# Seven half-size products for the Fourier half of an output projection, and reciprocal columns as matmul weights, in a two-block transformer kernel

## The reference, cut to what matters

```python
def second_block(x, c, ctx, c_ctx, norm_g, w_ada, b_ada, w_in, w_four, q_norm_g, k_norm_g, rel_bias, w_out):
    ...
        f_out = _fourier(fx_in, w_four[l]) * jax.nn.silu(fx_gate)
        na_out = _neighbourhood_attention(qx, kx, vx, kc, vc, rel_bias[l]) * jax.nn.silu(nx_gate)
        x_new = x + g_x * (jnp.concatenate([f_out, na_out], axis=-1) @ w_out[l])
```

## Time and profile before

| what | us |
|---|---|
| median of 3 runs (901.07 to 902.05) | 901.18 |
| profiled execution, its own time | 901.18 |
| its span, first to last instruction | 899.4 |
| TensorE busy | 887.7 (99%) |
| VectorE busy | 386.4 (43%) |
| ScalarE busy | 213.6 (24%) |
| GpSimd busy | 172.2 (19%) |
| step 4 of attention two, on TensorE | 816.1 to 829.7 |
| step 8's end, first product of the other half | 872.0 |

### The profile page before, as it was taken

One profiled execution on the slowest core, in us unless ns is written; L12 is line 12 of the kernel. 1 busy time (PEld: TensorE's weight loads), 2 busy tenths in 40 slices (PEclk: granted clock), 3 DMA queues, 4 the chain that ended last, 5 costly groups with the idle time before them and its releaser, 6 DMA issues.

```text
span 899.4 us, 13457 instructions
## 1 busy us (share of the span) xinstructions
PE 887.7 (99%) x5562; PEld 502.7 (56%) x5562; DVE 386.4 (43%) x814; ACT 213.6 (24%) x468; POOL 172.2 (19%) x160
## 2 busy tenths in 40 slices
PE   9999999999999989999999999999999999999998
PEld 5588875455565543333333333344688888866553
DVE  2764543357764346310310310048635542354456
ACT  2211213345544310010110110115201111643420
POOL 3212220000002044140230200033201303191000
PEclk9999999999999999999999999999999999999999
DMA  9945559124010738999999999961382102700002
GB/s 329 326 113 188 188 181 391 60 94 188 1 47 9 271 125 331 405 413 429 423 420 428 420 430 426 401 239 47 110 163 96 51 24 68 249 11 1 2 1 93
DMA packets 54830, 184.28 MB, mean 205 GB/s; under 512 B 15049, under 2 KB 15717, under 8 KB 48497
## 3 DMA queue, kind: packets, MB, share of 16 engines
q1 hardware_dynamic: 46368, 162.41, 48.0%
q0 software_dynamic: 4912, 14.18, 4.3%
q10 hardware_dynamic: 3488, 6.82, 2.0%
HBM read 168.70 MB, written 16.79 MB: 206 GB/s over the span
## 4 chain that ended last, share of the span: by engine, by line
PE 90%; DVE 3%; DMA 2%; ACT 2%; POOL 1%; issue 1%; SPq 0%; DVEq 0%; ACTq 0%; POOLq 0%
PE psum L981 20%; PE psum L1185 18%; PE psum L1206 9%; PE psum L1083 6%; PE psum L885 6%; PE psum L1031 4%; PE psum L1008 4%; PE psum L1457 3%; PE psum L1337 2%; PE psum L1299 2%; PE psum L1045 2%; PE psum L1062 2%; PE psum L1406 2%; PE psum L1110 2%; PE psum L944 1%
## 5 line engine op out<-in xcount | busy, mean ns | idle before, releaser
L1185 PE MATMUL psum<-ring,buf_a 128*32 128x512 f32 x1536 | 166.4, 592 | 1.6 <-issue 1.6
L1185 PEld LDWEIGHTS psum<-ring,buf_a 128*32 128x32 f32 x1536 | 51.6, 110 | 112.8 <-issue 112.8
L1206 PE MATMUL psum<-ring,buf_c 128*32 128x512 f32 x768 | 84.1, 593 | 0.0
L2718 POOL DMA_INDIRECT buf_b<-xq_d,o_sb x48 | 52.6, 1096 | 157.5 <-DVE buf_a L2300 125.1
L2649 POOL TENSOR_TENSOR qk_st<-qk_st,half 128x8 f32<-128x8 f32 x26 | 43.6, 1677 | 160.2 <-DVE qk_st L2384 74.5
L2325 DVE TENSOR_TENSOR buf_c<-buf_c,psum 128x512 f32<-128x512 f32 x12 | 13.1, 1093 | 141.0 <-PE psum L1185 141.0
L981 PE MATMUL psum<-ring,buf_a 128*128 128x256 f32 x320 | 70.9, 380 | 0.0
L981 PE MATMUL psum<-ring,buf_b 128*128 128x256 f32 x288 | 64.8, 380 | 0.0
L981 PEld LDWEIGHTS psum<-ring,buf_a 128*128 128x128 f32 x320 | 60.1, 190 | 8.2 <-issue 0.4
L1948 DVE TENSOR_TENSOR s_buf<-s_buf,psum 128x512 f32<-128x512 f32 x52 | 35.3, 685 | 61.2 <-PE psum L981 58.7
L981 PEld LDWEIGHTS psum<-ring,buf_b 128*128 128x128 f32 x288 | 53.9, 190 | 7.5 <-issue 0.6
(11 more groups left out here) (319 smaller groups left out, 1229.9 us busy)
## 6 DMA issues: line engine op xcount, KB each, us to landing
ring<-in_moe_w_gate SPq DMA_DIRECT2D x16, 2048.0 KB, 13.7
ring<-in_moe_w_up SPq DMA_DIRECT2D x16, 2048.0 KB, 14.8
ring<-in_moe_w_down SPq DMA_DIRECT2D x16, 2048.0 KB, 13.9
ring<-in_w_in SPq DMA_DIRECT2D x7, 2048.0 KB, 12.5
ring<-in_w_ada SPq DMA_DIRECT2D x6, 2048.0 KB, 9.8
ring<-in_da_w_in SPq DMA_DIRECT2D x5, 2048.0 KB, 14.4
y_d<-ring POOLq DMA_DIRECT2D x1, 5632.0 KB, 22.0
y_d<-buf_b ACTq DMA_DIRECT2D x11, 512.0 KB, 11.5
```

The source lines that it names most:

```text
L1185: last = mm(buf("mm", n)[rows, :], x_part[:, j, k, :], slot(moe_load(q, m, r))[:, k, :], start=(k == 0), stop=(k == KD - 1))
L1206: last = mm(buf("sc", n)[rows, m, :], hidT[:, s % 3, f * P + SUB * j:f * P + SUB * (j + 1)], slot(moe_load(q, 2, r), FC)[:, f, m * CH:(m + ...
L2718: pool.indirect_dma_start(out=xg[:, s % 2, j * 256:(j + 1) * 256], out_offset=None, in_=xn_quarters, in_offset=bass.IndirectOffsetOnAxis(a ...
```

## The change

The Fourier half of the projection gets the same seven products as the other half. Six of them (`OUT_F`) take the places of the pieces of three tiles, two in each of the steps 4, 5 and 6; the seventh (S4 times B22) takes the place of the last tile, one matmul in each of the four pieces of two. The sums of inputs are made by VectorE in step 3, behind the last piece of `mixT` and ahead of `diag` 1; the sums of weights by GpSimd at the same signal, `drained` of `fourier` 4 and 5. VectorE adds the products to the quarters of `x`: twelve instructions of 128 x 1024 in place of four, and one more that makes u2 out of the first product, which ScalarE has copied, and the fourth. The diagonal matrix is gone: `spread` now takes the reciprocal of one head as a 128 x 64 weight (one column, repeated) and the identity as the moving matrix, in eight matmuls of 128 columns in place of two of 512.

```diff
 BEFORE_PT = [[], [("fourier", 2)], [("fourier", 4)], [("fourier", 5)],
-             [("out_f", 0)], [("out_f", 1)], [("out_f", 2)], [("out_last", 0)], []]
+             [("out_f", 0)], [("out_f", 2)], [("out_f", 4)], [("out_last", 0)], []]
 AMID_PT = [[("fourier", 1)], [("fourier", 3)], [("fourier_rest", 4)], [("fourier_rest", 5)],
-           [("out_f_rest", 0)], [("out_f_rest", 1)], [("out_f_rest", 2)], [("out_last", 1)], []]
+           [("out_f", 1)], [("out_f", 3)], [("out_f", 5)], [("out_last", 1)], []]
+OUT_F = [("A11", "B11"), ("A12", "B21"), ("S3", "T3"), ("S2", "T2"), ("A22", "T4"), ("S1", "T1")]
...
+        def out_f(i):
+            n = turn["sc", "out_f", i]
+            left, right = OUT_F[i]
+            claim(pe, "sc", n)
+            if i == 2:
+                pe.wait_ge(s_f_ready, 1)
+                pe.wait_ge(t_f_ready, 2)
...
+            for a in range(2):
+                for k in range(2):
+                    last = mm(buf("sc", n)[:, a, :], mix_f[left][:, k, a * P:(a + 1) * P], w_out_f[right][:, k, :],
+                              start=(k == 0), stop=(k == 1))
+            fill(last, "sc", n)
...
         def out_last(piece):
...
-            for i in range(*OUT_LAST[piece]):
-                a, k = divmod(i, 4)
-                last = mm(buf("sc", n)[:, a, :], mixT[:, k, t * P:(t + 1) * P], gated_chunk(a)[:, k, :],
-                          start=(k == 0), stop=(k == 3))
+            a, k = divmod(piece, 2)
+            last = mm(buf("sc", n)[:, a, :], mix_f["S4"][:, k, a * P:(a + 1) * P], w_out_f["B22"][:, k, :],
+                      start=(k == 0), stop=(k == 1))
...
                 elif name == "spread":
...
-                    for hh in range(2):
-                        last = mm(buf("tp", n)[hh * DH:(hh + 1) * DH, :], ones[:, 0:DH],
-                                  o_sb[:, hh * 512:(hh + 1) * 512], start=True, stop=True)
+                    for g in range(4):
+                        for hh in range(2):
+                            last = mm(buf("tp", n)[hh * DH:(hh + 1) * DH, g * P:(g + 1) * P],
+                                      rden[:, m % 2, 2 * g + hh:2 * g + hh + 1].to_broadcast([P, DH]), ident[:], start=True, stop=True)
...
+                elif name == "out_f" and m == 0:
+                    act.wait_ge(f_added, 1)
+                    n = turn["sc", "out_f", 0]
+                    S.copy(f_p1, buf("sc", n)).then_inc(f_p1_copied, 1)
...
+        def sum_f(n):
+            left, right, op = {1: ("A21", "A22", ALU.add), 2: ("S1", "A11", ALU.subtract),
+                               3: ("A11", "A21", ALU.subtract), 4: ("A12", "S2", ALU.subtract)}[n]
+            if n == 2:
+                dve.wait_ge(s_f_ready, 2)
+            elif n == 4:
+                dve.wait_ge(s_f_ready, 3)
+            V.tensor_tensor(mix_f[f"S{n}"], mix_f[left], mix_f[right], op).then_inc(s_f_ready, 1)
...
+            elif i == 3:
+                dve.wait_ge(f_p1_copied, 1)
+                drain(V.tensor_tensor(f_u2, f_p1, product, ALU.add), "sc", n)
...
+            elif i == 5:
+                dve.wait_ge(f_added, 5)
+                add_to("x22", product).then_inc(f_added, 1)
+                drain(add_to("x12", product), "sc", n)
...
                 elif name == "fourier_rest":
...
+                    if m == 5:
+                        drained(dve, "sc", turn["sc", "fourier", 4])
+                        drained(dve, "sc", turn["sc", "fourier", 5])
+                        for sum_of in (3, 1, 2, 4):
+                            sum_f(sum_of)
...
                 elif name == "diag":
-                    link(V.reciprocal(rden[:, m % 2, :], rden[:, m % 2, :]))
-                    if m > 0:
-                        dve.wait_ge(mix_ready, m)
-                    V.tensor_tensor(rden_diag, ident[:].unsqueeze(1).unsqueeze(1).to_broadcast([P, 2, 4, P]),
-                                    rden[:, m % 2, :].rearrange("p (g h) -> p h g", h=2).unsqueeze(3).to_broadcast([P, 2, 4, P]),
-                                    ALU.mult).then_inc(rden_ready, 1)
+                    V.reciprocal(rden[:, m % 2, :], rden[:, m % 2, :]).then_inc(rden_ready, 1)
...
+        drained(pool, "sc", turn["sc", "fourier", 4])
+        drained(pool, "sc", turn["sc", "fourier", 5])
+        G.tensor_tensor(w_out_f["T1"], w_out_f["B12"], w_out_f["B11"], ALU.subtract).then_inc(t_f_ready, 1)
+        pool.wait_ge(t_f_ready, 1)
+        G.tensor_tensor(w_out_f["T3"], w_out_f["B22"], w_out_f["B12"], ALU.subtract).then_inc(t_f_ready, 1)
+        G.tensor_tensor(w_out_f["T2"], w_out_f["B22"], w_out_f["T1"], ALU.subtract).then_inc(t_f_ready, 1)
+        pool.wait_ge(t_f_ready, 3)
+        filled(pool, "sc", turn["sc", "out_f", 0])
+        G.tensor_tensor(w_out_f["T4"], w_out_f["B21"], w_out_f["T2"], ALU.subtract).then_inc(t_f_ready, 1)
```

More of the change, by code:

```diff
@@ L403, in build @@
     t_out = [ring[:, 2, n * 1024:(n + 1) * 1024].rearrange("p (k n) -> p k n", k=2) for n in range(4)]
-    s_out = [buf_d[:, n * 512:(n + 1) * 512].rearrange("p (k n) -> p k n", k=2) for n in range(4)]
+    s_out = [buf_d[:, n * 512:(n + 1) * 512].rearrange("p (k n) -> p k n", k=2) for n in range(4, 8)]
+    s_f = [buf_d[:, n * 512:(n + 1) * 512].rearrange("p (k n) -> p k n", k=2) for n in range(4)]
+    t_f = [ring[:, 5, n * 1024:(n + 1) * 1024].rearrange("p (k n) -> p k n", k=2) for n in range(2)]
+    f_p1, f_u2 = (buf_d[:, n * 1024:(n + 1) * 1024].rearrange("p (a n) -> p a n", a=2) for n in (2, 3))
     part = {"c11": s_buf[:, 0, 0, :], "c22": s_buf[:, 0, 1, :], "c21": s_buf[:, 1, 0, :], "c12": s_buf[:, 1, 1, :]}
@@ L563, in build @@
         w_out_part[f"B1{a + 1}"], w_out_part[f"B2{a + 1}"] = w[:, 4:6, :], w[:, 6:8, :]
+    mix_f = {"A11": mixT[:, 0:2, 0:HALF], "A12": mixT[:, 2:4, 0:HALF], "A21": mixT[:, 0:2, HALF:SEQ],
+             "A22": mixT[:, 2:4, HALF:SEQ], **{f"S{n + 1}": s_f[n] for n in range(4)}}
+    w_out_f = {f"T{n + 1}": t_f[n] for n in range(2)}
+    for a in range(2):
+        w = ring[:, slot_of[f"w_out{a}"][0], :].rearrange("p (k n) -> p k n", k=KD)
+        w_out_f[f"B1{a + 1}"], w_out_f[f"B2{a + 1}"] = w[:, 0:2, :], w[:, 2:4, :]
+    w_out_f["T3"], w_out_f["T4"] = w_out_f["B12"], w_out_f["B11"]
     x_part = {f"x{i + 1}{a + 1}": x[:, 2 * i:2 * i + 2, a * CH:(a + 1) * CH] for i in range(2) for a in range(2)}
@@ L1329, in _ @@
             seven_products(1, j)
[L1331 to L1337, removed]
-                          start=(k == 0), stop=(k == 3))
-            if a == 1:
-                fill(last, "sc", n)
+        def out_f(i):
[6 more added lines that the diff above has]
+            elif i == 3:
+                pe.wait_ge(s_f_ready, 3)
+                pe.wait_ge(t_f_ready, 3)
+            elif i == 4:
+                pe.wait_ge(t_f_ready, 4)
+            for a in range(2):
+                for k in range(2):
+                    last = mm(buf("sc", n)[:, a, :], mix_f[left][:, k, a * P:(a + 1) * P], w_out_f[right][:, k, :],
+                              start=(k == 0), stop=(k == 1))
+            fill(last, "sc", n)
         def out_last(piece):
-            n, t = turn["sc", "out_f", TT - 1], TT - 1
+            n = turn["sc", "out_f", len(OUT_F)]
             if piece == 0:
                 claim(pe, "sc", n)
-            for i in range(*OUT_LAST[piece]):
-                a, k = divmod(i, 4)
-                last = mm(buf("sc", n)[:, a, :], mixT[:, k, t * P:(t + 1) * P], gated_chunk(a)[:, k, :],
-                          start=(k == 0), stop=(k == 3))
+                pe.wait_ge(s_f_ready, 4)
+            a, k = divmod(piece, 2)
+            last = mm(buf("sc", n)[:, a, :], mix_f["S4"][:, k, a * P:(a + 1) * P], w_out_f["B22"][:, k, :],
+                      start=(k == 0), stop=(k == 1))
             if piece == 3:
                 fill(last, "sc", n)
[L1354 to L1358, removed]
         drained(pe, "tp", turn["tp", "qkT2", len(QK2) - 2])
@@ L1409, in _ @@
                         fill(last, "sc", n)
-                elif name in ("out_f", "out_f_rest"):
-                    if (name, m) == ("out_f", 0):
+                elif name == "out_f":
+                    if m == 0:
+                        pe.wait_ge(w_out_gated, 2 * KD)
                         drained(pe, "sc", turn["sc", "fourier", 4])
                         drained(pe, "sc", turn["sc", "fourier", 5])
-                    out_products(turn["sc", "out_f", m], m, 0 if name == "out_f" else 1)
+                    out_f(m)
                 elif name == "out_last":
@@ new lines, in add_to, with add_out_f @@
+        def add_to(part_of_x, product):
+            rows = x_part[part_of_x]
+            return V.tensor_tensor(rows, rows, product, ALU.add)
+        def add_out_f(i):
+            n = turn["sc", "out_f", i]
+            product = buf("sc", n)
+            if i == 4:
+                drained(dve, "sc", turn["sc", "out_f", 3])
+                dve.wait_ge(f_added, 2)
+                add_to("x21", f_u2).then_inc(f_added, 1)
```

(30 more changed lines are left out.)

16 lines of the change are left out of this document (7 added, 9 removed).

## The result

The changed kernel takes **907.69 us**, the median of 4 runs (907.08 to 908.23), beside 901.52 for the kernel before, also 4 runs (901.07 to 902.05) on the same chip: 1.0069 times as long, with a 95% interval of 1.0053 to 1.0085. The forecast was 907.0. The profiled execution took 907.35 us, with a span of 905.6.

A forecast was written before the change was run, and what follows sets the result against it. TensorE, busy 887.7 of 899.4 us, was taken to bound the kernel. The terms -3.5 - 0.45 + 7.55 + 0.05 + 1.6 + 0.5 + 0.05 gave +5.8, so 907.0 us; stated range 899.4 to 908.5.

The forecast's parts named there:

- Products: Last product's pieces on TensorE: 28 matmuls in place of 32, saving 3.5 us.
- Spread: Reciprocal spread on TensorE: eight 128-column matmuls cost the same as two of 512, so 0 us.
- rival C: Spread's head pairs do not overlap on TensorE: up to 3.7 us on top, 910.7 us; chance 0.03.
- The diagonal: VectorE's diagonal goes, ending TensorE's wait ahead of spread 0: -0.45 us.
- Sums of inputs, sums of weights: VectorE and GpSimd alternate sums in step 3, so TensorE stands still 7.55 us before spread 1.
- rival A: VectorE's sums run through without GpSimd getting between, ahead of spread 1: 899.5 us (899.2 to 899.8); chance 0.20.
- After the stop: TensorE runs slower after standing still before spread 1: +1.6 us, bounds 0 and 3.2.
- Adds: Sixth product's two adds free their buffer late for step 7's second scores: +0.5 us.
- The end of step 8: The last piece is one matmul, so the other half's first product waits for VectorE's gate: +0.05 us.
- Rival B: Only one or two GpSimd sums get between VectorE's sums before spread 1: 901.0 to 904.8 us; chance 0.10.

The follow-up runs named there:

- The kernels with no, one and two turns: Changed kernel, GpSimd's weight sums held until VectorE's reciprocal: all four, all but T1, all but T1 and T3; 899.21, 903.1, 905.22 us.
- the memsets: Changed kernel with four GpSimd zero fills beside VectorE's sums, GpSimd's own sums held until after the reciprocal; one execution 899.48 us.
- the last two kernels: Changed kernel with VectorE's input sums moved behind the first product's add, 897.47 us; the same with step 6's two products also swapped, 897.0 us.

## Why the prediction was right, step by step

The sum was +5.8, and +6.2 was measured in both the medians and the profiled spans. The step that carries it, the turns and the wait for the last S, is shown by the experiments; the largest error of a step is 0.3 us, for the clock, and that price came out as near as it did with some luck. The steps, in their own order:

- **Products:** forecast -3.5. By the starts, TensorE is 9.5 us late when the last product's first piece begins (869.86, against 860.34 before), and 6.1 us late behind the last one. That is -3.4, 0.85 a matmul, with the end of step 8 in it.
- **Spread:** forecast 0, measured 0.01 us a spread, alone and in the change. The 3.7 us of the upper bound, rival C, did not come.
- **The diagonal:** forecast -0.45, measured -0.48 at spread 0. That it would also have lengthened the stop, had it stayed, was not in the sum and did not need to be.
- **Sums of inputs, sums of weights:** forecast a stop of 7.55 us by three turns. Measured 7.57, with S3 at 0.69 us, S1 at 2.84, S2 and S4 at 2.71, where 0.7 and near 2.9 were forecast; T1, T3 and T2 were stretched by 0.3 to 0.5 us. The kernels with no, one and two turns show that this is the mechanism. The sharing that rival A spoke of falls: A's time, 899.2 to 899.8, comes only with GpSimd's sums held back until VectorE's are done (899.21, and 899.48 with the memsets). That two instructions exclude each other does not say who comes next, and a GpSimd that gives way each time, the other half of A, could not be excluded by the earlier trace rows. That GpSimd has the next turn rested on the earlier trace rows alone, and the runs bear it out.
- **After the stop:** forecast 1.6 us, with bounds of 0 and 3.2. Measured: spread 1 and values take 4.66 us instead of 2.78, so 1.9. This is the step that was chosen, not read, and its weak point was the clock column, 1.00 over the whole of the trace before. The price came from the earlier trace rows, where the column reads 1.00 too; what slowed those records no run shows, so that their price fits is in part luck. Nor is it one price: the profiled execution and one other have a mean granted clock of 0.996 (907.35 and 907.08 us), the other two 0.994 (908.04 and 908.23). After the long stop the column reads 0.50; in the kernel with a stop of 1.4 us the mean granted clock is 0.999 to 1.000 in all eight executions. The Trainium skill, TensorE: Matmul & The Clock Gate, "What's actually happening", states that an idle engine is throttled to 1.2 GHz. The trace agrees after the long stop (0.50).
- **Adds:** forecast +0.5. The wait in step 7 is 0.50 us in the row; by the starts, 0.7 us is lost and 0.2 comes back, so +0.5.
- **The end of step 8:** forecast +0.05, and as much at the first product; no wait is to be seen at either.

Rival B is what the kernels with one and two turns are. Its 901.0 to 904.8 stands against 903.1 and 905.22, the second just outside: the stop of two turns was 5.55 us where B had 5.35, and 1.84 us were lost behind it where B allowed 1.6. With one turn the clock was kept in three executions and lost in seven, so that B's range for it was needed.

The stop, the clock and the adds cost 7.6 + 1.9 + 0.5 = 10.0 us and the change saves 3.4 + 0.5 = 3.9: that is the whole result, 6.1 of the 6.2 us. The saving itself was there all along, as the last two kernels show: 4.0 us faster than before, with the same products.

## What to carry to other kernels

Before two engines are given elementwise work at one signal, look at whether both read two operands from SBUF. If so, expect them to take turns: here each instruction of GpSimd put off the end of VectorE's list by 2.0 to 2.1 us, and the price of 6.2 us (7.57 against 1.38) was that of the three of GpSimd's sums that met them. Put sums that nobody needs yet behind the instruction that somebody waits for, even if the engine looks idle where they stand. And a stop of several us in TensorE can cost more than its length, as here 1.9 us on 7.6.

## What the runs showed of the chip that was not expected

- GpSimd got its turn every time, between VectorE instructions that follow each other without a wait: three times in the changed kernel, with 2.71 to 2.84 us for the VectorE sum each time. The forecast rested on one such meeting and on two tiny instructions at the start of the span.
- With a stop of 3.5 us the time itself was uncertain: ten executions of the one-turn kernel lie between 901.22 and 904.6, where eight of the kernel without turns lie between 898.93 and 899.77. That the stop is the reason is likely and not shown.
- The clock fell at different points of the stop. With three turns it still reads 1.00 from 820 to 822 (above). With two turns, where the stop begins at much the same time, it is at 0.54 there. What is lost behind the stop is much the same, 1.84 and 1.88 us. The rows of the kernel with two turns:

```profile
820.00:822.00 2.00, 0.00 (x0) 0.54 0.00 0
822.00:824.00 2.00, 0.86 (x8) 0.50 0.00 0
```
